# Summing modulation panels in pairs, moving some of them between stages, and computing 28 of the input projection's x tiles as three products of rounded operands

## The reference, cut

```python
mod = silu(c) @ w_mod + b_mod                      # 6 x 1024 values, one row
h   = rmsnorm(x, g_mix) * (1 + mod[1]) + mod[0]
p   = h @ w_in      # 256 x 1024 by 1024 x 5632: f_f f_b i_in q og u v ga gb
# recurrence over chunks of 64 rows, 4 heads; gating of u by a mixed layernorm(v)
merged = sigmoid(ga) * (o_a @ w_pa) + sigmoid(gb) * (o_b @ w_pb)
x   = x + mod[2] * (merged @ w_o)
x   = x + mod[5] * swiglu(modulate(rmsnorm(x), mod[3], mod[4]))
# second part: mod_w_2 (2 layers x 6144 columns) and kv_mod_w_2 (2048 columns) are used
# in the same way, each for one row c_2
y   = sum over experts of gate * gelu(h . u_e) * v_e        # PEER
```

## Time and profile before

| | |
|---|---|
| three runs | 2589.7, 2584.69, 2582.22 us; median 2584.69 |
| profiled execution | 2585.32 us, span of its instructions 2583.5 |
| mean granted TensorE clock | 0.987 |
| busy share | TensorE 97%, weight loads 87%, VectorE 69%, ScalarE 48% |
| chain that ended last | TensorE 86%, VectorE 6%, DMA 1%, ScalarE 1% |
| HBM read | 468.51 MB, 182 GB/s over the span |
| stages, us from the start | mixer to 359, up 366, down 498, GLA 572, first PEER 727 (values 1216.6 to 1577.0), window attention 1588, second PEER from 1720 (values from 2208.6) |

### The profile page before, as it was taken

One profiled execution on the slowest core, in us unless ns is written; L12 is line 12 of the kernel. 1 busy time (PEld: TensorE's weight loads), 2 busy tenths in 40 slices (PEclk: granted clock), 3 DMA queues, 4 the chain that ended last, 5 costly groups with the idle time before them and its releaser, 6 DMA issues.

```text
span 2583.5 us, 43038 instructions
## 1 busy us (share of the span) xinstructions
PE 2500.4 (97%) x15948; PEld 2246.5 (87%) x15948; DVE 1780.5 (69%) x3565; ACT 1239.6 (48%) x2429; POOL 79.4 (3%) x42
## 2 busy tenths in 40 slices
PE   7999999999999999999999998989999999999997
PEld 4587889988889999999888887789999999888886
DVE  5672668866359977786788875739987787555554
ACT  2322124432234567775444444433557776455444
POOL 0000000000050000000000000022000000000000
PEclk9999999999999999999999999999999999999998
DMA  6562567656343554444777764233554444555553
GB/s 265 197 243 82 204 221 278 237 219 228 115 144 137 181 179 138 141 146 151 259 279 275 274 233 162 82 115 115 180 181 150 144 142 140 193 195 192 190 191 110
DMA packets 65352, 471.70 MB, mean 183 GB/s; under 512 B 7296, under 2 KB 7552, under 8 KB 8240
## 3 DMA queue, kind: packets, MB, share of 16 engines
q1 hardware_dynamic: 64656, 467.85, 50.5%
q10 hardware_dynamic: 272, 1.05, 0.1%
q0 software_dynamic: 272, 0.69, 0.1%
HBM read 468.51 MB, written 1.05 MB: 182 GB/s over the span
## 4 chain that ended last, share of the span: by engine, by line
PE 86%; DVE 6%; DMA 1%; ACT 1%; issue 1%; DVEq 0%; SPq 0%; ACTq 0%
PE bank L745 27%; PE bank L670 27%; PE bank L902 5%; PE bank L682 4%; PE bank L532 4%; PE bank L811 4%; PE bank L697 3%; PE bank L933 2%; PE bank L996 1%; PE bank L542 1%; PE bank L1039 1%; DVE macc L1686 1%; PE bank L516 1%; PE bank L809 1%; PE bank L548 1%
## 5 line engine op out<-in xcount | busy, mean ns | idle before, releaser
L670 PE MATMUL bank<-h_split,t_split 128*128 128x256 f32 x6144 | 772.2, 285 | 6.2 <-DVE t_split L1918 4.9
L670 PEld LDWEIGHTS bank<-h_split,t_split 128*128 128x128 f32 x6144 | 745.5, 191 | 8.5 <-DVE t_split L1918 6.1
L1918 DVE TENSOR_TENSOR t_split<-ring,t_split 128x1024 fp32r<-128x1024 f32 x512 | 624.7, 1221 | 160.7 <-ACT t_split L1212 159.3
L745 PE MATMUL bank<-t_split,w_split 128*128 128x512 f32 x3072 | 703.9, 390 | 0.0
L745 PEld LDWEIGHTS bank<-t_split,w_split 128*128 128x128 f32 x3072 | 574.8, 188 | 118.8
L1217 ACT ACTIVATE t_split<-ring 128x1024 fp32r<-128x1024 f32 x256 | 271.6, 1061 | 357.8 <-PE bank L745 288.7
L1212 ACT ACTIVATE t_split<-ring 128x1024 fp32r<-128x1024 f32 x256 | 271.1, 1059 | 295.8 <-PE bank L670 275.2
L1950 DVE TENSOR_TENSOR w_split<-arena,w_split 128x256 fp32r<-128x256 f32 x256 | 108.8, 425 | 223.5 <-ACT w_split L1219 223.5
L1139 ACT ACTIVATE arena<-bank 128x256 f32<-128x256 f32 (+2 forms) x160 | 64.3, 405 | 326.6 <-PE bank L697 67.0
L1686 DVE SCALAR_TENSOR_TENSOR macc<-ring,cact,macc 128x256 f32<-128x256 f32 x336 | 162.9, 485 | 12.0
L902 PE MATMUL bank<-h_split,wd_split 128*128 128x256 f32 x1056 | 130.1, 284 | 4.0 <-ACT h_split L1439 4.0
(11 more groups left out here) (302 smaller groups left out, 2768.9 us busy)
## 6 DMA issues: line engine op xcount, KB each, us to landing
ring<-in_peer_u SPq DMA_DIRECT2D x128, 1024.0 KB, 4.9
ring<-in_peer_v SPq DMA_DIRECT2D x128, 1024.0 KB, 4.9
ring<-in_w_mod SPq DMA_DIRECT2D x24, 1024.0 KB, 5.1
ring<-in_mod_w SPq DMA_DIRECT2D x24, 1024.0 KB, 4.9
arena<-in_mod_w SPq DMA_DIRECT2D x24, 1024.0 KB, 6.5
ring<-in_w_in SPq DMA_DIRECT2D x22, 1024.0 KB, 4.9
ring<-in_w_up SPq DMA_DIRECT2D x22, 1024.0 KB, 5.1
ring<-in_peer_wq SPq DMA_DIRECT2D x16, 1024.0 KB, 4.9
```

The costliest lines, as they stand in the source:

```text
L670: last = mm(bank[:, 0:T], u[:, a_, k, :], h_split[:, b_, k, :], start=(k == 0 and a_ + b_ == 0), stop=(k == KT - 1 and a_ == 1))
L745: last = mm(BK[2 * tt + hf][:, :], w_split[:, j, a_, tt * P:(tt + 1) * P], t_split[:, 1 - j, b_, hf * 512:(hf + 1) * 512], start=(first an ...
L1918: TT(t_split[:, 1 - j, 1, :].rearrange("p (k c) -> p k c", k=KT), ring[:, r, :].rearrange(view, k=KT, j=2)[:, j], t_split[:, 1 - j, 0, :]. ...
```

## The change

Four things change.

1. **Sums in pairs, folded at the end.** `mod_between` takes two neighbouring panels in one instruction (2 x 256 columns), so 8 instructions for both; at the last one `mod_acc` rises by two and frees both slots. VectorE then transposes the sums in 32 x 32 blocks and adds each row of 32, and writes 4 x 2 values a panel and partition to a new buffer `quad`. The turns (lines 502 and 772) go. Instead `mod_fold` on TensorE sums `quad` once for a group of panels: four plain float32 matmuls with a 128-column window of `fold`, a matrix of shifted identities made at the start. There are five folds, of 14, 18, 28, 8 and 4 panels. Single panels are still summed in the up, down and GLA stages, with the transposition and the reduction behind each.
2. **Panels moved.** The pair of `w_mod` behind the fourth `w_in` panel, and the single ones, are regrouped; no modulation panel stands among `w_pab` and `w_o`. `mod_w0`'s last eight stand in GLA, and `kv_mod`'s eight with the first 20 of `mod_w1` in the value stage of the first PEER layer (14 pairs, `V_PAIRS`), the last four in that of the second (2 pairs).
3. **Where they land.** In the value stages pairs are loaded to `H` in quarters, `v_mod`: two transfers of 256 KB each (512 columns of each of two panels), eight for a pair. The first eight are issued ahead of the third value panel, behind a new wait of SyncE for `proj`. VectorE does one paired step a block, eight a pair.
4. **x tiles of panels 2 to 15 in three products.** ScalarE's new `hi_x(p)` rounds the panel into `xin_hi` (two buffers, on the place of `cum0`, `cum1`), VectorE's new `lo_x(p)` writes the remainder over the panel in its ring slot, and the slot is free only after TensorE's third product. `Hx` is split once into `x_split` (on the place of `fg0`, `fg1`), behind a new semaphore `x_free`.

The core of the diff, TensorE and VectorE:

```diff
-    + [(a["w_in"], 1, "proj", 2), (a["w_mod"], 2, "mod_acc", 1)] * 4
+    + [(a["w_in"], 1, "proj", 2), (a["w_mod"], 2, "mod_acc", 1)] * 3
+    + [(a["w_in"], 1, "proj", 2)]
     + [(a["w_in"], 1, "proj", 4), (a["w_mod"], 2, "mod_acc", 1)] * 2
-    + [(a["w_in"], 1, "proj", 2), (a["w_mod"], 1, "mod_acc", 1)] * 4
+    + [(a["w_in"], 2, "proj", 2), (a["w_mod"], 2, "mod_acc", 1)] * 2
     + [(a["w_in"], 10, "proj", 2)]
-    + [(a["w_in"], 1, "proj", 2), (a["mod_w0"], 1, "mod_acc", 1)] * 2
-    + [(a["w_pab"], 1, "proj", 4), (a["mod_w0"], 1, "mod_acc", 1)] * 4
-    + [(a["w_o"], 1, "proj", 2), (a["mod_w0"], 1, "mod_acc", 1)] * 2
-    + [(a["w_o"], 2, "proj", 2)]
+    + [(a["w_in"], 1, "proj", 2), (a["w_mod"], 1, "mod_acc", 1)] * 2
+    + [(a["w_pab"], 4, "proj", 4), (a["w_o"], 4, "proj", 2)]
...
+            def mod_fold(panels):
+                if e.refill("mod_bank"):
+                    pe.wait_ge(sems["mod_bank"], e.freed("mod_bank"))
+                pe.wait_ge(sems["mod_quad"], e.more("mod_quad", panels))
+                for w in range(4):
+                    last = mm(BK[6][:, 0:2 * panels], fold[:, 96 - 32 * w:224 - 32 * w],
+                              quad[:, 0:panels, :, w], start=(w == 0), stop=(w == 3))
+                last.then_inc(sems["mod_turn"], 1)
...
+                        pe.wait_ge(sems["xin_hi"], 2 * (p - XF) + 2)
+                        if p == XF:
+                            pe.wait_ge(sems["x_hi"], 2)
+                            pe.wait_ge(sems["x_lo"], 2)
...
+                    for w, b_ in ((wh, 0), (wh, 1), (wl, 0)):
+                        if w is wl and m % 2 == 0:
+                            pe.wait_ge(sems["xin_lo"], p - XF + 1)
+                        for k in range(KT):
...
+            def lo_x(p):
+                for j in range(2):
+                    part = slice(j * D, (j + 1) * D)
+                    dve.wait_ge(sems["xin_hi"], 2 * (p - XF) + j + 1)
+                    ins = TT(ring_lo[:, XIN[p] % RING, part], slot(XIN[p])[:, part], xin_hi[:, p % 2, part].bitcast(f32), SUB)
+                ins.then_inc(sems["xin_lo"], 1)
```

ScalarE, and VectorE's order in and around the heads (`behind` is called in `lin` when a head's state updates are done):

```diff
             for n in range(8):
                 evac("turn", M1["kN"][:, 0:T], ACT.Copy)
                 x_tiles(1)
-            x_tiles(4)
+                if n == 0:
+                    act.wait_ge(sems["x_free"], 1)
+                    for j in range(2):
+                        part = slice(4 * j, 4 * j + 4)
+                        A(x_split[:, 0, part, :], Hx[:, part, :], ACT.Copy).then_inc(sems["x_hi"], 1)
+                if n == 2:
+                    hi_x(2)
+                if n in (3, 5, 7):
+                    hi_x(3 + (n - 3) // 2)
+            x_tiles(2)
+            hi_x(6)
+            x_tiles(2)
             lin_turned(M1, 0, 2)
+            hi_x(7)
             x_tiles(1)
             for h in range(HEADS):
                 if h + 1 < HEADS:
                     lin_turned(M1, h + 1, 2)
                     x_tiles(1)
+                    hi_x(8 + h)
                 x_tiles(1)
...
+            def behind_head(h):
+                lo_x(8 + h)
+                if h == 2:
+                    ln_stats()
+                if h == 3:
+                    ln_apply()
+            lo_x(6)
+            lo_x(7)
+            lin(M1, 2, 1, M1["tB"], P, lambda d, h: S0[:, d, h, :], normed, behind_head)
+            lo_x(14)
```

More of the change, by code:

```diff
@@ new lines, in v_step @@
+                def v_step(i, at, used, src, n):
+                    for c in range(4):
+                        v_panel(i * 2 + (at + c // 2), c % 2)
+                        sync.wait_ge(sems["mod_used"], i * 4 + (used + c + 1))
+                        v_mod(src, i * 2 + n, c)
+                sync.wait_ge(sems["proj"], total["proj"] + BLOCKS)
+                src, n0 = (a["kv_mod"], 0) if layer == 0 else (a["mod_w1"], 20)
+                for c in range(4):
+                    v_mod(src, n0, c)
@@ new lines, in _ @@
+                for r in range(2):
+                    v_panel(0, r)
+                if layer == 0:
+                    with sync.Fori(0, 3) as i:
+                        v_step(i, 1, 0, a["kv_mod"], 2)
+                    with sync.Fori(0, 10) as i:
+                        v_step(i, 7, 12, a["mod_w1"], 0)
+                else:
+                    v_step(0, 1, 4 * V_PAIRS[0], a["mod_w1"], 22)
+                done = 2 * V_PAIRS[layer] - 1
+                with sync.Fori(0, PAIRS // 2 - 1 - done) as i:
+                    for r in range(2):
+                        v_panel(i + done, r)
@@ L1400, in x_tiles, with hi_x @@
                     tile_now[0] += 1
+            def hi_x(p):
+                m = XIN[p]
+                act.wait_ge(sems[f"loaded{m % RING}"], 16 * (m // RING + 1))
+                for j in range(2):
+                    part = slice(j * D, (j + 1) * D)
+                    A(xin_hi[:, p % 2, part], slot(m)[:, part], ACT.Copy).then_inc(sems["xin_hi"], 1)
             for n in range(8):
@@ L1690, in mod_between @@
-                    ins.then_inc(sems["mod_acc"], 1)
-            def mod_out(first, cols, bias, dst=modc):
+                    slots.append(r)
+                wrapped = n == 2 and slots[1] < slots[0]
+                part = ring[:, 0:RING:RING - 1, :] if wrapped else ring[:, slots[0]:slots[0] + n, :]
+                w = part.rearrange("p s (k c) -> p s k c", k=KT)
+                acc, turned = macc[:, 0:n, :], (nrm[:, 0:2, :] if n == 2 else macc[:, 1:2, :])
+                TS(acc, w[:, :, 0, :], cact[:, c_col:c_col + 1], None, MUL).then_inc(sems["dve_step"], 1)
@@ L1783, in normed @@
                 oT = kt(M1["oT"], 4)
-                roots(root_buf, dv)
+                dve.wait_ge(sems["oms"], e.more("oms"))
+                for pair in range(2):
+                    ins = TS(root_buf[:, pair * 512:(pair + 1) * 512], BK[pair][:, :], 1.0 / dv, EPS, MUL, ADD)
+                ins.then_inc(sems["ovar"], 1)
+                dve.wait_ge(sems["ostd"], e.more("ostd"))
+                dve.reciprocal(root_buf[:, 0:512], root_buf[:, 0:512])
+                lo_x(12)
+                dve.reciprocal(root_buf[:, 512:1024], root_buf[:, 512:1024]).then_inc(sems["dve_step"], 1)
+                lo_x(13)
+                dve.wait_ge(sems["dve_step"], e.stepped())
                 for h in range(HEADS):
@@ L2117, in _ @@
                 TT(chunks(M1[f"ki{d}"]), chunks(M1[f"ki{d}"]), k4, MUL)
-                TT(chunks(M1[f"kd{d}"]), chunks(M1[f"kd{d}"]), k4, MUL)
-            used(1)
-            mod_between(1, 0)
-            used(1)
-            mod_between(1, 0)
+                ins = TT(chunks(M1[f"kd{d}"]), chunks(M1[f"kd{d}"]), k4, MUL)
+            ins.then_inc(sems["x_free"], 1)
+            used(2)
+            mod_between(2, 0)
+            for j in range(2):
+                part = slice(4 * j, 4 * j + 4)
+                dve.wait_ge(sems["x_hi"], j + 1)
+                TT(x_split[:, 1, part, :], Hx[:, part, :], x_split[:, 0, part, :].bitcast(f32), SUB).then_inc(sems["x_lo"], 1)
+            lo_x(2)
             S0 = M1["S0"].rearrange("p (d h n) -> p d h n", d=2, h=4)
@@ L2190, in _ @@
             ins.then_inc(sems["sgu"], 1)
+            lo_x(15)
             e.tiles("proj", 4)
```

338 lines of the change are left out of this document (163 added, 175 removed).

## The result

| | before | after |
|---|---|---|
| median (lowest to highest), 8 runs each | 2584.8 (2581.8 to 2589.7) | 2594.9 (2590.6 to 2602.5) |
| span of the profiled execution | 2583.5 | 2593.3 |
| mean granted TensorE clock | 0.987 | 0.976 |

The ratio is 1.0040 (95% interval 1.0026 to 1.0054): the changed kernel is 10 us slower. I had forecast 7 us faster, with 2590 as the upper end of the range.

The account below looks back on a forecast made before the run. TensorE, busy 97% of the span, was taken as the bound. From 2585.3 us, terms -6.5 + 5.3 + 9.9 - 4.6 + 9 - 6.0 - 4.2 - 1.8 - 10.3 + 1.7 = -7.5 gave 2577.8; range 2563 to 2590 (0.8).

Parts of the forecast that it names:

- The clock: x tiles and heads: half clock behind three 5.8 us waits at 2.7 each, 1 for waits near 3.7; +9 (0 to +14).
- Waits of 1.3 to 2.4 leave the clock at 1.00: TensorE: claimed such short waits leave the clock full; offered in support of the rival where the clock holds.
- rival B: x tiles and heads: the same waits, but the clock holds; 9 less, 2568.8 us (2560 to 2573); chance 0.20.
- Value stages' start: Each value stage: modulation loads ahead of the third value panel delay it; 0 to 2 us, taken 0.8.
- Up to the first x tile: Start to first x tile: turns and weight waits go, TensorE there at 138.0 instead of 144.7; -6.5 us (-7 to -3).
- Tiles 0 to 11, waits alone: x tiles 0 to 11: new waits of 3.8, 3.6, 3.8 and tile 10, 11.6 us together; whole stretch +5.3.
- Heads, waits alone: Four heads: VectorE's remainders delay state updates, three waits of about 5.8 us, one with 2.05 more; stretch +9.9 (+4 to +12).
- Tiles 19 to 31, output projections, up and down, GLA: Later mixer stages: rounded tiles -4.6, output projections -6.0, up and down -4.2, GLA -1.8 us.
- F: Modulation sums on VectorE: pairing isn't cheaper, a step costs twice 485 ns; +5, 2583 us; chance 0.05.
- Rival D: Value stages: the quarter loads are slow, 16 rounds each 2.5 us longer at 150 GB/s; +40, 2618 us; chance 0.07.
- Rival E: Heads: the ring of four slots stays behind, another 3.7 us at each of four panels; +15, 2593 us; chance 0.08.
- C: x tiles: panels ready in time, terms 5.3, 9.9 and 9 become -6, -6 and 0; 2541 us; chance 0.12.

Follow-up runs that it names:

- split_from_6: Changed kernel, but x panels 2 to 5 plain and x's two parts made later (tile 4, behind panel 5's modulation pair): 2576.4 us, 0.9969.
- value_first: Changed kernel, but at both value stages' start value panel 2 is issued ahead of the eight quarter loads, panel 3 behind the first pair of quarters: 2588.7 us, 1.0018.
- spread_quarters: Changed kernel, but at both value stages' start each value panel is issued ahead of one pair of quarter loads: 2583.3 us, 0.9992.
- combined_6: Changed kernel with split_from_6, late_remainders and spread_quarters in one: 2550.2 us, 0.9857.
- combined_6_again: The same kernel as combined_6, run again on the chip: 2545.2 us, 0.9850.
- late_remainders: Changed kernel, but in the heads the remainders of panels 7 to 11 and the layer norm statistics stand behind the state updates on VectorE: 2574.8 us, 0.9959.
- plain_tiles: Changed kernel, but all 16 x panels multiplied as plain float32, without splitting of x: 2564.5 us, 0.9924.

## Why the prediction was wrong

The two mechanisms that decide the sign, waits by the order of instructions and half clock behind them, were in the forecast, in the right places. The step that failed is the price of two terms: the half clock behind the waits of tiles 0 to 11, put at 1 us (9 measured), and the late landing of value panel 2 at the start of each value stage, put at 0.8 us (6.2 and 4.3 measured). A third term, the stretch up to the first x tile, missed by 3 us to the same side.

- **The clock: +9 forecast, about 17 measured.** The working gave 2.7 us to each of three waits in the heads, and 1 us to all waits near 3.7. The first part was right: 8.1 against 7.4. The second failed. In tiles 0 to 11 the changed kernel loses 18.0 us against split_from_6; its waits are 13.8 (11.3 and 2.5), eight rounded tiles win 5.0, so 9.2 is half clock. The rows say the same: the products behind the waits of 4.05, 3.68, 3.56 and 1.89 take 2.9, 2.9, 1.8 and 1.3 us longer than at full clock, 8.9 in all., in the forecast itself, showed a wait of 4.0 that cost 3 us, so the number for a wait of this length stood in the trace; for the 1 us no row was given.
- **"Waits of 1.3 to 2.4 leave the clock at 1.00" did not hold even in the kernel before.** It holds for the waits of 1.30 in its heads. But its product behind a wait of 1.77 takes 5.20 where the ones around it take 3.62, and a stretch within it shows the clock at 0.50:

```profile
36.96 5.20 PE L475 MATMUL bank<-ring,cact 128*2 128x256 f32 x16 [1.77 <-DMA ring<-in_w_mod]
```

```profile
38.00:40.00 2.00, 2.00 (x6) 0.60 (x5) 1.86 (x5) 0.00 (x0) 0.00 (x0) 0.50 1.07 425
```

  The waits of 2.30 at 51.57 and of 2.16 at 1579.13 are followed by 0.50 as well. So the sentence gave rival B support that it did not have, and it let the short new waits pass at no price.
- **Value stages' start: 0.8 each forecast, 6.2 and 4.3 measured.** -10.3 came out as -4.9 and +1.7 as +7.0. I priced the later issue of value panel 2, and for its slower landing wrote only "three in flight land later". It landed 9.3 us after issue, not 4.9, behind 2 MB of quarters. value_first and spread_quarters give the size: 4.8 and 4.0 us for the first reorder, 6.2 and 4.3 for the second. What is left fits in the first peer: 351.4 against 362.5 is -11.1, where 12.0 less a fold of 0.9 was forecast. In the second 2.6 is left for a fold of 1.0; 0.98 of the rest is the last wait, and 0.7 stays open.
- **Up to the first x tile: -6.5 forecast, -3.4 measured.** The row below, before the second half of the context projection, is new.

```profile
97.23 15.70 PE L539 MATMUL bank<-H,ring 128*128 128x512 f32 x32 [2.28 <-DMA ring<-in_w_in]
```

  In the kernel before, two turns ahead of it kept TensorE busy until 97.44, so this panel's landing was hidden by work that was then taken away. The product behind the wait takes 15.70, where value_first has 14.00 behind the same wait (2.23): clock again, in this profile. The panels' landing times were walked through only for the first x panel, not for this one. No run was made for it; it is argued from the rows.
- **Tiles 0 to 11, waits alone: right.** 11.6 of new waits forecast, 13.8 there, by the causes named (`x_free` behind tile 0: 3.8 forecast, 4.05; `hi_x(3)`: 3.6 and 3.68; `hi_x(4)`: 3.8 and 3.56). The rest of the difference is tile 10: 0.4 is left for it in the sum, and its wait was 1.89.
- **Heads, waits alone: right.** Three waits 5.8 forecast, one with 2.05 more; 5.55, 5.55 and 7.52 measured.
- **Tiles 19 to 31, output projections, up and down, GLA: right or better**, by 0.6 to 2.9 us. At the last down panel I had a wait growing to 2.1; there is none, the fold at 570.58 follows the products without a gap, and so does the panel behind it.
- **The pairing: right.** A paired step takes 0.745 us (0.75 forecast), transpose and reduction 0.71 and 0.69 (0.7 each), so F falls. VectorE in the first peer's value stage, 1245 to 1570 us (count, busy us, mean ns):

```profile
L2067 DVE SCALAR_TENSOR_TENSOR macc<-H,cact,macc 128x512 f32<-128x512 f32 x98 | 73.0, 745 | 0.0
...
L2076 DVE STREAM_TRANSPOSE nrm<-macc 128x512 f32<-128x512 f32 x14 | 10.0, 711 | 0.5
L2078 DVE TENSOR_REDUCE quad<-nrm 128x512 f32 x14 | 9.6, 686 | 2.0
```

- **Rival D is out behind the stages' start, and half right in it.** In the first peer TensorE has no wait for a load from 1245 to 1584 us, and 96 products, eight blocks, take 21.9 us, where 21.8 was forecast (1464 take 333.47). ScalarE does wait for value panels, 46 times, 69.8 us in all and at most 1.9 (5.9 us in four waits in the kernel before), and all of it is covered. The Trainium skill asks for 1 MiB or more for 75% of peak (DMA: Bandwidth & Descriptors, section Bandwidth). Behind the start no run shows a loss by the smaller transfers: the queues move 267 GB/s on average, with 1 MB and 256 KB transfers mixed. At the start the trace does point that way:

```profile
1226.00:1231.00 5.00, 5.00 (x24) 4.12 (x23) 3.16 (x7) 3.01 (x5) 0.00 (x0) 1.00 0.74 237
1231.00:1236.00 5.00, 5.00 (x24) 4.14 (x23) 2.33 (x3) 1.37 (x2) 0.00 (x0) 1.00 0.88 266
1236.00:1241.00 5.00, 0.93 (x5) 0.43 (x3) 0.00 (x0) 0.91 (x1) 0.00 (x0) 1.00 0.94 392
```

  In the first 10 us most packets are the quarters' (1113 of 1174 are under 8 KB, the size of a value panel's), in the last 5 most are the value panels' (228 of 309). A quarter lands 5.1 us after its issue, a whole panel of four times its bytes 4.9 (medians of the whole kernel). So the quarters kept panel 2 back, as value_first shows, by their bytes and, as these rows suggest, by a slower pace while they ran among themselves. How much the size of a transfer has to do with that pace was not tried.
- **Rival E** (+15 from the ring) gave the measured time to within 2 us, but not by its mechanism: in the heads nothing of TensorE waits for a load, and VectorE's waits there are for roundings that wait for TensorE's own tile. Rival B is out by the clock, C by the waits.

The range ended at 2590. Three terms passed their own upper ends: the clock (+14) by about 3 us, the value stages (-8 and +3) by 3 and 4. With 3 us behind each of the six long waits, as the earlier trace rows has it, the clock would have been +18 and the forecast 2587.

## What to carry to other kernels

A step that prepares an operand costs what stands behind it in its engine's queue, not its own length: place a rounding or a remainder behind what another engine waits for, and check that the load it needs lands ahead of its turn. Count a long TensorE wait (3.6 to 7.5 us here) as the wait and 2 to 3 us of half clock behind it, do not take a wait of 1.3 to 2.4 as free, and take these numbers from a row of the same kernel. When transfers are put ahead of others, add their bytes to the landing time of the first one behind them, most of all at a stage's start, where there is no lead yet.

## What the runs showed of the hardware that I had not expected

- Work without use made the kernel faster: 40 float32 products in the waits of three heads, 18.1 us of TensorE's time, took 8 us off (2594.9 to 2586.7), 7.5 of them in these heads and nearly all of that through the clock.
- The same wait can cost the clock in one execution and not in the next. The wait for a `w_in` panel near 97 us is in the profile of the changed kernel and in all eleven of its variants' (2.14 to 2.44 us), ahead of the same 32 products. Six show them at 15.70 us, six at 14.00, and of two profiles of one kernel combined_6 has 15.70 (wait of 2.25) and combined_6_again 14.00 (wait of 2.31). So a difference of 1.7 us between two profiles can be this alone.
- A wait of 1.30 us was followed by a slow product (3.11 us for 2.17) twice in combined_6, at the same two places in two runs, and by none in late_remainders, plain_tiles and the kernel before with waits of the same length in their heads. The kernels differ in which of the tiles ahead are rounded. What decides it stays open.
- Quarter loads of 256 KB, mixed with panels of 1 MB, kept the queues at 267 GB/s on average through the first value stage (1245 to 1584 us) with no wait of VectorE for them; eight of them in a row ran at about 250 GB/s (1226 to 1236 us), and the panels behind them at 392.
